# First stage of a two-layer decoder step on one core: cached tokens compressed beside the conditioning, requests from two engines, first weights split in between, token tiles turned one tile later

## The reference, cut to what matters

```
mod = (silu(c) @ ada_w + b)                      # conditioning: 6 vectors of 1024 per sequence
h   = rms_norm(x) * (1 + scale) + shift          # scale, shift out of mod
qa, ka, va, qb, kc, vc, ks, vs, kw, vw, gates = split(h @ w_in)   # rope on q and k
kcc = silu(blocks(cached k) @ cmp_w1[0]) @ cmp_w2[0]    # 32 tokens, stride 16; the same for v
vcc = silu(blocks(cached v) @ cmp_w1[1]) @ cmp_w2[1]    # with cmp_w1[1], cmp_w2[1]
```

## Time and profile before

| | |
|---|---|
| median of 3 runs | 1903.7 us (1898.15 to 1910.28) |
| the profiled execution | 1904.86 us, span 1903.2 us |
| busy share | PE 94%, DVE 47%, ACT 24%, POOL 4% |
| chain that ended last | PE 89%, DVE 7%, ACT 1%, DMA 1% |
| granted PE clock, mean | 0.94 of full |

### The profile page before, as it was taken

How to read it: one execution, slowest core, us unless ns; L and a number is a source line. 1 busy time by engine, 2 the same in 40 slices (tenths; PEclk the granted TensorE clock), 3 DMA queues, 4 the chain that set the end, 5 groups by cost and what they waited for, 6 DMA issues and landing times.

```text
span 1903.2 us, 32761 instructions
## 1 busy us (share of the span) xinstructions
PE 1788.3 (94%) x14212; PEld 1630.2 (86%) x14212; DVE 889.6 (47%) x1650; ACT 465.1 (24%) x746; POOL 78.5 (4%) x146
## 2 busy tenths in 40 slices
PE   5979999999999899999999899878988999999998
PEld 3768888777768899999999897767878999999997
DVE  3534243344344653636353523376565745454442
ACT  1512221134463311111111324122322311111112
POOL 2000001500030000000000000000000000000000
PEclk7889999989999999999999999877779999999998
DMA  9657665410062222222223465122232222222211
GB/s 352 227 196 248 223 199 166 177 51 1 23 223 90 67 79 78 88 88 87 67 88 126 146 199 177 46 70 70 70 120 89 67 89 72 82 88 88 78 54 50
DMA packets 160179, 218.83 MB, mean 115 GB/s; under 512 B 7271, under 2 KB 131198, under 8 KB 159630
## 3 DMA queue, kind: packets, MB, share of 16 engines
q1 hardware_dynamic: 148814, 177.52, 28.4%
q0 software_dynamic: 11264, 39.86, 6.0%
HBM read 199.66 MB, written 21.76 MB: 116 GB/s over the span
## 4 chain that ended last, share of the span: by engine, by line
PE 89%; DVE 7%; ACT 1%; DMA 1%; issue 1%; SPq 0%; ACTq 0%; DVEq 0%
PE ps L1365 14%; PE ps L1363 14%; PE ps L1362 14%; PE ps L1041 4%; PE ps L1042 4%; PE ps L1043 4%; PE ps L918 3%; PE ps L1151 2%; PE ps L1328 2%; PE ps L1329 2%; PE ps L1331 2%; PE ps L1137 2%; PE ps L967 1%; PE ps L1166 1%; PE ps L1459 1%
## 5 line engine op out<-in xcount | busy, mean ns | idle before, releaser
L1362 PE MATMUL ps<-arena_r,wring_r 128*128 128x288 f32 x2048 | 570.1, 293 | 7.4 <-DVE hbuf_r L2131 7.4
L1365 PE MATMUL ps<-arena_r,wring_r 128*128 128x288 f32 x2048 | 439.6, 296 | 0.0
L1362 PEld LDWEIGHTS ps<-arena_r,wring_r 128*128 128x128 f32 x2048 | 386.0, 188 | 7.7 <-issue 7.7
L1365 PEld LDWEIGHTS ps<-arena_r,wring_r 128*128 128x128 f32 x2048 | 328.3, 188 | 0.0
L1363 PE MATMUL ps<-hbuf_r,wring_r 128*128 128x288 f32 x1024 | 286.1, 295 | 0.0
L1363 PE MATMUL ps<-arena_r,wring_r 128*128 128x288 f32 x1024 | 284.6, 294 | 0.0
L1833 ACT ACTIVATE wring_r<-wring 128x2048 fp32r<-128x2048 f32 x64 | 122.5, 1917 | 620.5 <-DMA wring<-in_mlp_w 620.5
L1363 PEld LDWEIGHTS ps<-hbuf_r,wring_r 128*128 128x128 f32 x1024 | 193.9, 189 | 0.0
L1363 PEld LDWEIGHTS ps<-arena_r,wring_r 128*128 128x128 f32 x1024 | 192.4, 188 | 0.0
L2469 DVE SCALAR_TENSOR_TENSOR xbuf<-ps,mod,xbuf 128x288 f32<-128x288 f32 (+1 forms) x128 | 56.1, 480 | 245.5 <-PE ps L1365 245.5
L1041 PE MATMUL ps<-wring_r,xbuf_r 128*128 128x512 f32 x360 | 149.9, 416 | 0.0
(11 more groups left out here) (378 smaller groups left out, 2627.2 us busy)
## 6 DMA issues: line engine op xcount, KB each, us to landing
wring<-in_mlp_w SPq DMA_DIRECT2D x64, 1024.0 KB, 5.2
arena<-in_ada_w SPq DMA_DIRECT2D x40, 1024.0 KB, 5.8
wring<-in_even_w_in SPq DMA_DIRECT2D x14, 1024.0 KB, 8.2
wring<-in_gla_w_in SPq DMA_DIRECT2D x12, 1024.0 KB, 5.6
wring<-in_ada_w SPq DMA_DIRECT2D x4, 2048.0 KB, 28.1
xbuf<-xspill SPq DMA_DIRECT2D x2, 2304.0 KB, 9.3
arena<-in_cache_cmp_kv POOLq DMA_DIRECT2D x16, 256.0 KB, 10.1
wring<-in_cache_diff_k POOLq DMA_DIRECT2D x16, 256.0 KB, 3.6
```

Of the source, the lines that this page charges most:

```text
L1362: pe.matmul(bank, hi, x_hi[:, k, cols], start=k == 0, stop=False)
L1365: mm = pe.matmul(bank, lo, x_hi[:, k, cols], start=False, stop=k == KC - 1)
```

## The change

Seven edits, all in the stage above.

1. **Requests.** The cache pages 0 to 7 are requested by POOL, each right after its own page number is read; pages 8 to 15 by ACT, in the same manner, before ACT's first computation. One semaphore per four pages takes the place of one for all. On SP the samples go ahead of x; the large constants go behind the first projection weights and the store of x; the first compression weights go ahead of the conditioning weights, the second too, but only after the squares are summed.
2. **x.** The samples are turned first, ahead of the prompt's chunks, and the squares are taken as the chunks come, into another buffer. silu(c) and lambda no longer stand ahead of the root on ACT.
3. **Pages of the keys** are turned right after (two groups before) the spreading, with DVE's copies between its multiplications; then the keys are compressed.
4. **Conditioning steps 0 to 3** stand between the value pages' groups on all three engines; the first half of the value compression follows, then steps 4 to 7, then the second half.
5. **First weights.** Units 0 and 1 are rounded and split between conditioning steps; units 2 and 3 inside the projection's loop, as the later ones are.
6. **Turns.** PE turns tile u - 2 at the end of unit u instead of tile u - 1. ACT's list is unchanged here: `keep_turn(u - 1)` at the end of its unit u.
7. Semaphores of the prompt's compression are merged with those of the samples'.

```diff
+            load_cmp(0)
+            sp.wait_ge(norm_sum, 1)
+            load_cmp(1)
             for n in range(WSLOTS):
                 load(W_ADA0 + n, ada0(n))
-            load_cmp(0)
-            load_cmp(1)
-            sp.wait_ge(x_evac, KC + 1)
-            sp.dma_start(xspill, xbuf[:, 0:KC * T]).then_inc(x_spilled, 16)
             def load_unit(n, src, k=KC):
@@ -709,6 +705,10 @@
                     load_unit(W_IN + 2 * j + i, src, 4)
             load_in(0)
+            sp.wait_ge(x_evac, KC + 1)
+            sp.dma_start(xspill, xbuf[:, 0:KC * T]).then_inc(x_spilled, 16)
+            sp.dma_start(cf[:, first:], a["const_f32"][:, first:]).then_inc(const_loaded, 16)
+            sp.dma_start(cb[:, :], a["const_bf16"]).then_inc(const_loaded, 16)
             sp.dma_start(gwin[:, :, :], a["even_w_in"][0].rearrange("(k p) c -> p k c", p=P)[:, :, 3584:3596]).then_inc(gcols_loaded, 16)
             load_in(1)
             sp.wait_ge(cmp_mm, 2)
...
             cmp_pages = a["cache_cmp_kv"][0].rearrange("f t v g d -> f t (v g d)")
+            page = []
             for m in range(NS * NPAGE):
-                pool.dma_start(ctok[:, m, :], cmp_pages[bass.ds(page[m], 1)].rearrange("o t c -> (o t) c")
-                               ).then_inc(ctok_loaded, 16)
+                page.append(pool.value_load(pagesb[0:1, m:m + 1], min_val=0, max_val=a["cache_diff_k"].shape[1] - 1))
+                if m < NS * NPAGE // 2:
+                    pool.dma_start(ctok[:, m, :], cmp_pages[bass.ds(page[m], 1)].rearrange("o t c -> (o t) c")
+                                   ).then_inc(ctok_loaded[m // 4], 16)
             pool.wait_ge(cmp2_kept, 1)
             pool.wait_ge(x_evac, KC + 1)
...
+                q, c = PAGE_ORDER[i], 8 * v + i
+                g, pair = q // 4, q % 4
+                if v == 0:
+                    pe.wait_ge(ctok_loaded[pair], 16 * 4)
+                if c < 3:
+                    pe.wait_ge(x_evac, KC + 1)
+                else:
+                    pe.wait_ge((cxs_act, cxs_dve)[(c - 3) % 2], (c - 3) // 2 + 1)
+                for w in range(4):
+                    n, pg = 2 * pair + w // 2, w % 2
+                    mm = pe.transpose(ps[:, page_bank(c), w * P:(w + 1) * P],
+                                      ctok[:, n * NPAGE + pg, (2 * v + g) * P:(2 * v + g + 1) * P], ident[:, :])
+                mm.then_inc(ctok_turned, 1)
+            def compress_samples(v, part, parts):
...
@@ -996,16 +1001,23 @@
             pe.wait_ge(x_evac, KC + 1)
             pe.wait_ge(small_kept, 3)
             norm_sums(0)
+            turn_page(0, 0)
+            turn_page(0, 1)
             norm_spreads(0)
+            for i in range(2, 8):
+                turn_page(0, i)
+            compress_samples(0, 0, 1)
             pe.wait_ge(cexp_ready, 2)
             pe.wait_ge(ada_zero, 1)
-            for x in range(EARLY):
+            for i in range(8):
+                turn_page(1, i)
+                if i % 2:
+                    ada_early(i // 2)
+            compress_samples(1, 0, 2)
+            for x in range(4, EARLY):
                 ada_early(x)
             ada_fold(EARLY - 1)
-            turn_pages(0)
...
                                 mm = pe.matmul(ps[0:NS * NB_S, 5, g * P:(g + 1) * P], hids[:, 1, g * NS * NB_S:(g + 1) * NS * NB_S],
                                                cw2[:, 1, :], start=True, stop=True)
                     mm.then_inc(cmp2_mm, 1)
-                if u:
-                    turn(u - 1)
+                if u >= 2:
+                    turn(u - 2)
                 if 1 <= u <= LATE[0] + 1:
                     ada_late(0, u - 1)
+            turn(len(pj_units) - 2)
             turn(len(pj_units) - 1)
             pe.wait_ge(pj_dve, dve_upto[-1])
             pe.wait_ge(pj_act, act_upto[-1])
+            pe.wait_ge(const_loaded, 32)
...
             def cmp_exps(v):
                 act.wait_ge(cmp_exp, v + 1)
                 act.activation(hids[:, v, :], hids[:, v, :], ACT.Exp, scale=-1.0).then_inc(act_chain, 1)
-            act.wait_ge(x_evac, KC + 1)
-            act.wait_ge(small_turned, 1)
-            squares(0, x_evac, 0)
+            act.wait_ge(pages_loaded, 16)
+            cmp_pages = a["cache_cmp_kv"][0].rearrange("f t v g d -> f t (v g d)")
+            for m in range(NS * NPAGE // 2, NS * NPAGE):
+                at = act.value_load(pagesb[0:1, m:m + 1], min_val=0, max_val=a["cache_diff_k"].shape[1] - 1)
+                act.dma_start(ctok[:, m, :], cmp_pages[bass.ds(at, 1)].rearrange("o t c -> (o t) c")
+                              ).then_inc(ctok_loaded[m // 4], 16)
+            squares(0, x_evac, 1)
+            act.wait_ge(lam_ready, 1)
+            norm_root(0)
             act.wait_ge(small_kept, 2)
             act.activation(cexp, v2T[:, V2_C:V2_ROWS], ACT.Exp, scale=-1.0).then_inc(cexp_ready, 1)
-            act.wait_ge(lam_ready, 1)
+            for i in range(0, 8, 2):
+                keep_page(0, i)
             act.activation(lam[:, 2:4], lam[:, 0:2], ACT.Exp).then_inc(lam_ready, 1)
-            norm_root(0)
-            for x in range(EARLY):
-                ada_keep(x)
-            keep_pages(0)
+            act.wait_ge(cmp_mm, 1)
+            for i in range(0, 8, 2):
+                keep_page(1, i)
+                ada_keep(i // 2)
+            cmp_exps(0)
             def round_unit(n, k=KC):
                 raw, high, _ = unit(n, k)
                 act.wait_ge(w_ready[n % WSLOTS], fills(n))
                 act.activation(high, raw, ACT.Copy).then_inc(w_high, 1)
+            for n in range(2):
+                round_unit(W_IN + n, 4)
+            for x in range(4, EARLY):
+                ada_keep(x)
             def round_h(dst, chunks):
...
+                if j < 6 and t in (2, 3):
                     round_unit(W_IN + 2 * (j + 1) + t - 2, 4)
...
                 ins = dve.tensor_tensor(hT[:, k, 0:SEQ], xT[:, k, 0:SEQ], ps[:, 4, :], ALU.mult)
-            step(ins)
-            for x in range(EARLY):
+                if k in (2, 4, 6):
+                    keep_page(0, k + 1)
+            ins.then_inc(norm_x, 1)
+            dve.wait_ge(lam_ready, 2)
+            step(dve.tensor_tensor(lam[:, 4:5], lam[:, 3:4], lam[:, 2:3], ALU.subtract))
+            dve.tensor_scalar(lam[:, 5:6], lam[:, 4:5], -LAM_INIT, None, ALU.add).then_inc(lam_ready, 1)
+            dve.wait_ge(cmp_mm, 1)
+            pe_columns(1)
+            for i in range(1, 8, 2):
+                keep_page(1, i)
+                if i > 1:
+                    ada_add(i // 2 - 1)
+            cmp_sums(0)
+            rest_unit(W_IN, S_IN, 4)
+            for x in range(3, EARLY):
                 ada_add(x)
+                if x == 3:
+                    cmp_silu(0)
+                elif x == 4:
+                    rest_unit(W_IN + 1, S_IN + 1, 4)
             dve.wait_ge(ada_kept, EARLY)
             mod_scale(0, v1T[:, V1_N1:V1_N1 + KC])
-            dve.sem_inc(norm_x, KC)
-            keep_pages(0)
+            dve.sem_inc(norm_x, KC - 1)
             step(dve.tensor_tensor(hs_seq, hs_seq, by_sequence(modA), ALU.mult))
             dve.tensor_tensor(hs_seq, hs_seq, by_sequence(mod[:, 0:KC, :]), ALU.add).then_inc(norm_x, 1)
             rest_samples(xT_r, H_IN)
             for k in range(KC):
                 dve.wait_ge(h_high, H_IN + k + 2)
                 dve.tensor_tensor(hT_r[:, k, 0:SEQ], hT[:, k, 0:SEQ], xT_r[:, k, 0:SEQ].bitcast(F32), ALU.subtract).then_inc(h_split, 1)
-            dve.wait_ge(cmp_mm, 1)
-            pe_columns(1)
-            keep_pages(1)
-            cmp_sums(0)
             def keep_compressed():
```

More of the change, by code:

```diff
@@ L333, in decoder_program @@
         cmpw_loaded = [sem(f"cmpw_loaded{i}") for i in range(2)]
-        ctok_loaded = sem("ctok_loaded")
+        ctok_loaded = [sem(f"ctok_loaded{i}") for i in range(4)]
         gcols_loaded = sem("gcols_loaded")
@@ L967, in compress_samples @@
+            def compress_samples(v, part, parts):
+                if part == 0:
+                    pe.wait_ge(cmpw_loaded[v], 16)
+                    pe.wait_ge(cxs_act, 4 * v + 4)
+                    pe.wait_ge(cxs_dve, 4 * v + 4)
+                    pe.wait_ge(pe_col, v + 1)
+                    pe.wait_ge(norm_x, 1) if v else pe.wait_ge(norm_std, 1)
+                for l in range(CL // parts * part, CL // parts * (part + 1)):
                     mm = pe.matmul(ps[:, 4 * v, 0:CROW - 1], cw1[:, v, l * P:(l + 1) * P], cxs[:, l % CS, l // CS:l // CS + CROW - 1],
@@ L1598, in ada_keep, with keep_page @@
                 act.activation(ada_row(x), ps[:, 6, 128:256], ACT.Copy).then_inc(ada_rows, 1)
[L1600 to L1606 removed]
+            def keep_page(v, i):
+                c = 8 * v + i
+                act.wait_ge(ctok_turned, c + 1)
+                act.activation(page_columns(PAGE_ORDER[i]), page_blocks(c), ACT.Copy).then_inc(cxs_act, 1)
             def cmp_exps(v):
@@ L1651, in _ @@
             modulate_first()
-            keep_pages(1)
```

(25 more changed lines are left out.)

147 lines of the change are left out of this document (54 added, 93 removed).

## The result

| | before | after |
|---|---|---|
| median, ten runs each | 1903.8 us (1898.15 to 1912.58) | 1917.1 us (1903.87 to 1921.81) |
| profiled execution | 1904.86 us | 1907.74 us |
| its granted clock, mean | 0.940 | 0.949 |

The ratio is 1.0057, with a 95% interval of 1.0035 to 1.008: about 11 us slower, within the 1% that was called no change. It is the ratio of the means, 1915.9 over 1905.0; the medians differ by 13.3. The forecast was 1904 with a range to 1916; the median lies 1.1 us above its top.

A forecast was written before the change was run, and what follows sets the result against it. PE was taken to bound the kernel, through its waits and lower clock. 1904.86 - 10.5 (first stage) - 11.0 (handover) - 1.0 (late piece) + 21.5 (later turn) = 1903.9, forecast as 1904 us, range 1895 to 1916.

The forecast's parts named there:

- What bounds the kernel: Whole kernel: PE holds 89% of the chain of waits, so only PE's waits and its lower clock count.
- First stage: Everything before the first pair of projection units: the pair starts sooner, 10.5 us gained, bounds 0 and 14.
- the open term: PE's clock in conditioning steps 4 to 7 and second half compression: a fall costs 4.7 us; the middle was taken.
- Handover: From the pair of units to the end of unit 2: no wait for the first rotated tile, 11.0 us gained.
- Late piece: PE's wait of about 1.8 us for a late conditioning piece at 134.9 us: 1.0 us gained, bounds -2 and 1.8.
- Later turn: Projection units 2 to 25: the fold waits for ACT's tile and row copies, 19 times, 21.5 us lost in sum.
- A: Rival on the projection loop: the later turn's wait is hidden, 1882 us; chance 0.12.
- B: Rival on the first stage: it gains nothing, ACT stuck in requests and clock low, 1914 us; chance 0.13.
- C: Rival on units 2 to 25: holes drop PE's clock, 2.7 us at each of 19 units, 1955 us; chance 0.05.

The follow-up runs named there:

- e1: Changed kernel with ACT's copy of the turned tile also moved one tile later; ratio to the kernel before 0.9948, median 1898.0 us.
- e5: Changed kernel with POOL's 4 MB window store moved from before the loop to unit 28; ratio to the kernel before 1.002.
- e7: Changed kernel with all 16 pages requested by POOL and none by ACT; ratio to the kernel before 1.0039.
- e3: Kernel before with the later turn alone (PE turns tile u - 2 at the end of unit u); ratio to the kernel before 1.0078.
- e2: Changed kernel with the later turn undone (PE turns tile u - 1 again), the rest kept; ratio to the kernel before 0.9988.
- e6: Changed kernel with both ACT's copy one tile later and the window store moved to unit 28; ratio to the kernel before 0.992.
- e4: Changed kernel with two more ACT copies ahead of each late conditioning row of layer 0, lengthening the holes; ratio to the kernel before 1.011.
- e8: Kernel before with six more 128x128 turns near the start of PE's list; ratio to the kernel before 1.0149, +27 us in medians.
- e12: Changed kernel with 128 semaphore increments at the start of PE's list; ratio to the kernel before 1.0046.
- e9: e6 with all pages requested by POOL; ratio to the kernel before 0.9886, median 1883.4 us.

## Why the prediction was right, and where it fell short

**What bounds the kernel**: right. PE holds 89% of the chain after as before.

**First stage**: the parts held, the open term fell well. Squares 15.3 (18.0 forecast), root 25.3 (24.2), spreading 29.3 (28.4), compression 37.3 for 15.8 (36.6 for 16.6), pair 82.9 (84.3). The clock, which had been at 0.50 among the same steps, stayed at 1.00 with compression in between, so the gain is 14.2, not the middle value of 10.5. By how much is in part chance: with the same code it is 11.1 in e1 and 15.3 in e5. The root came later than forecast although the squares started 2.7 sooner, because the sums waited for the small tensors (above), a wait that the working did not have; it held that nothing but x was waited for. That ACT asks for half the pages gained nothing (e7). What of the rest came from asking per page and what from the operations removed ahead of the root, no run separates. The rule of the Trainium skill cited there, that several requesters save only issue time, agrees with the trace: from 15 to 30 us the DMA share is 1.03 to 1.05 in after and 1.03 to 1.04 in e7, at 374 to 399 and 395 to 403 GB/s.

**Handover**: right, 25.5 - 14.2 = 11.3 against 11.0. e3 ends unit 2 10.9 sooner too, 0.9 of it from an earlier start.

**Late piece**: wrong in sign. +1.0 was forecast; in its place came a wait of 3.0 us and a clock fall behind it, against 1.8 before:

```profile
120.00:122.00 2.00, 0.04 (x1) 0.00 (x0) 0.91 (x3) 0.00 (x0) 0.00 (x0) 1.00 0.78 200
122.00:124.00 2.00, 0.97 (x20) 0.76 (x24) 0.00 (x0) 0.00 (x0) 0.00 (x0) 0.63 0.99 329
```

That unit took 12.76 us where its neighbours with the hole take 8.34 to 8.39, so 4.4 in place of 1.8: 2.6 lost. The prediction held that the piece stays where it was relative to POOL's copy. That was so: POOL asks for the copy at 97.29, 14.4 behind the pair's start, as it had at 111.58.

```profile
111.58 0.62 POOL L802 DMA_DIRECT2D out<-in_state_win_kv  x1
```

```profile
97.29 0.62 POOL L803 DMA_DIRECT2D out<-in_state_win_kv  x1
```

But the 11.3 us of the handover had been time in which the queues caught up. PE now ends unit 2 at 4.2 us behind that request, where it had been 15.4, and the copy takes 23 us to land in both. The removal of one wait was paid for in part by the next, and the working should have carried the 11.0 over to this term. In e1 and e2, whose units take less time, the wait is 6.7 and 7.7. With the copy moved (e5) it vanishes.

**Later turn**: right in mechanism, and nearly in size. Of the 27.4 us lost between 101.45 and the second mark, 2.6 are the late piece. A clock fall behind one hole of 1.51 us, the only one in 19, is 1.6 (9.95 us for that unit where e5, with the same hole, takes 8.35):

```profile
139.88 1.11 ACT L1695 ACTIVATE arena<-ps 64x64 f32<-64x64 f32 x8 [7.53 <-PE ps L1036]
141.35 0.40 PE L926 MATMUL ps<-cf,arena 128*128 128x18 f32 x2 [1.51 <-ACT arena L1612]
```

```profile
144.00:146.00 2.00, 2.00 (x7) 1.52 (x6) 0.00 (x0) 0.00 (x0) 0.00 (x0) 0.50 0.95 303
```

The rest, 23.2, is the toll; 21.5 was forecast from 19 terms, and e5 against e6 gives 23.1. The fold starts 1.45 us behind the turn, as priced (1.46). But a unit of the common kind grows by 1.11 us, from 7.23 to 8.34, where 1.03 was priced: the product behind the fold starts 0.33 after it instead of 0.23. e1 removes the toll, e3 makes it alone.

**Rivals.** A fell to the 19 rows. B fell to the pair's start. C: one fall of 1.6 us in 19 holes, and two in e4 with longer ones. By the Trainium skill's rule cited with it, that short idle times make the clock swing, there would have been many; at holes up to 2.1 us the trace here is against it. The wait of 3.0 did bring a fall.

**The sum.** In the profiled executions the change is +2.9 us against -1.0 forecast. The 3.9 between them are: first stage -3.7, handover -0.3, late piece +3.6 (2.6 and the 1.0 not gained), toll +1.7, the clock fall in the loop +1.6, later stages +1.0. That the profile came so near is partly luck: terms of up to 3.7 us cancel.

**The step that failed is the one from the profiled execution to the median.** I put the profile 1.2 above the median and carried that over. After's profiled execution lies 8.2 under the mean of its ten runs (1915.9) and 9.4 under their median, where before's lies on its mean (1905.0). Part of this is the clock. After's profiled execution had 0.949, its ten runs 0.9457 in the mean. How much 0.001 of mean clock is worth differs by the runs that are asked: 1.9 us in 26 runs of the kernel before that stood beside e1 to e4 (correlation -0.77), 1.0 in 23 beside e5 to e8 (-0.46), 1.1 in the ten of after (-0.60). So 3.3 x 1.0 to 1.9, or some 3 to 6 us of the 8.2, go with a clock that the profiled execution had and the others, on average, did not; the rest has no cause here. The +11 is then +2.9 of the sum above and these 8.2. The holes are not what keeps it low: e1, which has none before a fold, averages 0.9441, not more. Since only one execution has a trace, where the others lose it stays open: in the stages behind 360 us, as in e2, in the first stage, whose length varies by 4 us in the same code, in holes of the last loop such as e1's profile has, or in the place of the code, which e12 hints at.

## What to carry to other kernels

When work moves later on one engine, move its partner's turn in every other list too: here one line on ACT was worth 20 us, most of what the change had won. A wait at the head of an in-order queue is priced from rows of what stands between releaser and waiter, and that worked to within 2 us in 21.5 over 19 units. Before comparing two kernels at a per cent, hold the profiled execution's granted clock against that of all runs, and the count of instruction loads against the other kernel's; here the one went with some 3 to 6 us, the other with holes of 5 to 15 us.

## What the runs showed of the hardware

- Twelve more PE records near the head of the list cost 27 us, most of it 1400 us later, with instruction loads going from 76 to 103 and holes of up to 4.3 us in a loop. 128 increments at its head brought neither.
- Instruction loads and holes without a releaser in the last loop rise together: 76 or 77 with 3.8 us of holes, 85 with 9.2 and 9.8, 94 with 15.5 and 16.3, 103 with 18.6.
- Profiles of e1, e5 and e6 had 94, 94 and 85 instruction loads and lay 7.9, 11.4 and 7.5 us over their medians, but e4's had 85 and lay 4.8 under; those of e9 and e7 had 76 and lay 7.8 and 17.3 under. Whether the loads differ from run to run of one kernel stays open.
- 128 semaphore increments on PE let its first turn start at 20.46 us: at most 0.16 us each, an estimate that takes them to begin at 0. The pair starts only 8.4 to 9.4 us later, because PE had waited for x before (first turn at 5.2 in after and e9, 11.9 in before).
- Nineteen holes of 0.6 to 2.1 us left PE's clock at 0.97 or more in the mean of each 100 us; a later stage with falls of its own lasted from 128.3 to 136.8 us in one code.
